# Both attentions of a small transformer layer, on one core: each pair of heads begins with a plain score step of the next pair, and the shift is turned ahead of the small value product

## What is computed

```python
def blocked_causal_attention(q, k, v, scale, cum_log_f=None):
    ...
        s = jnp.einsum('bqhd,bkhd->bhqk', q_blk, k, preferred_element_type=jnp.float32) * scale
        if use_decay:
            s = s + fq[..., :, None] - f_bh[:, :, None, :]
        ...
        s = jnp.where(mask[None, None], s, NEG)
        p = jax.nn.softmax(s, axis=-1)
        return jnp.einsum('bhqk,bkhd->bqhd', p.astype(v.dtype), v)

def attention_mixer(h, ...):
    ...
    q = rope_tail(rms_norm(q, g_q_mla), cos, sin)
    k = rope_tail(rms_norm(k, g_k_mla), cos, sin)
    o_mla = blocked_causal_attention(pad_front(q), pad_front(k), pad_front(v_mla), MLA_QK ** -0.5)[:, PAD:]
    ...
    o_fox = blocked_causal_attention(pad_front(qf), pad_front(kf), pad_front(vf), FOX_DIM ** -0.5, cum_log_f)[:, PAD:]
    return jnp.concatenate([o_mla, o_fox], axis=-1) @ w_out
```

## Time and profile before

| | |
|---|---|
| median of 3 runs | 1785.78 us (1784.84 to 1786.84) |
| the profiled execution's own time | 1785.57 us |
| its span | 1783.8 us |
| mean granted TensorE clock | 0.976 |
| the two attentions, with the MLA projections between them | 141 to 341.7 us |

### The profile page before, as it was taken

How to read it: one execution, slowest core, us unless ns; L and a number is a source line. 1 busy time by engine, 2 the same in 40 slices (tenths; PEclk the granted TensorE clock), 3 DMA queues, 4 the chain that set the end, 5 groups by cost and what they waited for, 6 DMA issues and landing times.

```text
span 1783.8 us, 27270 instructions
## 1 busy us (share of the span) xinstructions
PE 1732.7 (97%) x11417; PEld 1505.6 (84%) x11417; DVE 885.8 (50%) x1193; ACT 633.5 (36%) x980; POOL 142.9 (8%) x151
## 2 busy tenths in 40 slices
PE   7999999999999999999999999999999999879998
PEld 6997767899999999999887888888877886667987
DVE  5534556464343434655665343434665476525362
ACT  4523444433231313221233232323344465542222
POOL 1000000040000000400031000000330000003100
PEclk9999999999999999999999999999999999967999
DMA  5240000022222222222222232322464660001001
GB/s 180 71 96 8 7 26 24 25 95 95 95 95 81 86 92 94 95 95 94 94 86 95 92 99 92 98 91 98 94 88 67 99 95 4 1 11 48 1 24 71
DMA packets 137545, 129.57 MB, mean 73 GB/s; under 512 B 17633, under 2 KB 135512, under 8 KB 137452
## 3 DMA queue, kind: packets, MB, share of 16 engines
q1 hardware_dynamic: 137250, 128.18, 26.2%
q10 hardware_dynamic: 202, 0.06, 0.0%
HBM read 126.14 MB, written 2.10 MB: 72 GB/s over the span
## 4 chain that ended last, share of the span: by engine, by line
PE 92%; ACT 3%; DVE 3%; issue 1%; SPq 1%; POOL 0%; DMA 0%; ACTq 0%; DVEq 0%; POOLq 0%
PE ps L430 71%; PE ps L859 3%; PE ps L756 1%; PE ps L1094 1%; PE ps L739 1%; PE ps L1880 1%; PE ps L2140 1%; PE ps L2150 1%; PE ps L2147 1%; PE ps L1159 1%; PE ps L2167 0%; PE ps L2175 0%; PE ps L764 0%; PE ps L2098 0%; PE ps L2100 0%
## 5 line engine op out<-in xcount | busy, mean ns | idle before, releaser
L403 ACT ACTIVATE w_hi<-raw 128x1024 fp32r<-128x1024 f32 (+1 forms) x227 | 239.3, 1055 | 818.9 <-PE ps L430 812.9
L430 PE MATMUL ps<-x_hi,w_hi 128*128 128x258 f32 (+4 forms) x1640 | 450.5, 327 | 3.7 <-DVE x_lo L450 2.8
L430 PE MATMUL ps<-x_lo,w_hi 128*128 128x258 f32 (+4 forms) x1640 | 444.3, 323 | 0.0
L430 PE MATMUL ps<-x_hi,w_lo 128*128 128x258 f32 (+4 forms) x1640 | 443.4, 323 | 0.0
L411 DVE TENSOR_TENSOR w_lo<-raw,w_hi 128x1024 fp32r<-128x1024 f32 (+1 forms) x227 | 294.7, 1299 | 98.6 <-ACT w_hi L403 98.5
L430 PEld LDWEIGHTS ps<-x_hi,w_hi 128*128 128x128 f32 (+2 forms) x1640 | 273.4, 188 | 34.7 <-issue 3.8
L430 PEld LDWEIGHTS ps<-x_lo,w_hi 128*128 128x128 f32 (+2 forms) x1640 | 272.3, 187 | 28.0 <-issue 2.4
L430 PEld LDWEIGHTS ps<-x_hi,w_lo 128*128 128x128 f32 (+2 forms) x1640 | 272.2, 188 | 25.8
L430 PE MATMUL ps<-a_hi,w_hi 128*128 128x258 f32 (+1 forms) x1024 | 281.0, 325 | 3.5 <-issue 3.2
L430 PE MATMUL ps<-a_hi,w_lo 128*128 128x258 f32 (+1 forms) x1024 | 280.9, 325 | 0.0
L430 PE MATMUL ps<-a_lo,w_hi 128*128 128x258 f32 (+1 forms) x1024 | 280.6, 325 | 0.0
(11 more groups left out here) (397 smaller groups left out, 1842.5 us busy)
## 6 DMA issues: line engine op xcount, KB each, us to landing
raw<-in_w_mlp_up SPq DMA_DIRECT2D x32, 1024.0 KB, 5.4
raw<-in_w_mlp_down SPq DMA_DIRECT2D x32, 1024.0 KB, 4.8
raw<-in_w_in SPq DMA_DIRECT2D x16, 1024.0 KB, 8.9
raw<-in_w_in_conv SPq DMA_DIRECT2D x12, 1024.0 KB, 5.1
raw<-in_w_in_attn SPq DMA_DIRECT2D x8, 1024.0 KB, 5.2
raw<-in_w_out_attn SPq DMA_DIRECT2D x4, 1024.0 KB, 4.9
raw<-in_w_out_conv SPq DMA_DIRECT2D x4, 1024.0 KB, 4.8
raw<-in_w_out SPq DMA_DIRECT2D x4, 1024.0 KB, 5.7
```

The costliest lines, as they stand in the source:

```text
L403: act.activation(dst, panel_view(p)[:, :, o:o + w], ACT.Copy).then_inc(w_hi_ok, 1)
L430: ins = pe.matmul(pair_of_banks[t % 2][0:m, b, 0:c], w[:, k, :], x[:, k, x0:x0 + c], start=(k == order[0] and n == 0), stop=(k == order[-1 ...
```

## The change

Only the list of steps on PE changes, in `fox_ring`, for pairs 1 to 3 and 4 to 7. Each pair begins with step 3 of the next pair's plain scores instead of its own turned step 0. All plain steps move ahead by one place. `lat` moves from behind the turned step 1 to behind the turned step 2. `bq` and `bk` keep their places behind turned steps 1 and 2, but what stands three places ahead of each changes. The turned step 3 moves behind `sm`, and `nt` comes ahead of `pm`. No instruction is added or taken away. The order on DVE, ACT, POOL and SP stays as it is.

```diff
     for c in range(1, 4):
-        body = [("u", c, 0), ("s", c + 1, 3), ("u", c, 1), ("lat", c - 1), ("s", c + 1, 2), ("u", c, 2), ("s", c + 1, 1), ("u", c, 3),
-                ("s", c + 1, 0), ("sm", c + 1), ("pm", c), ("nt", c + 1), ("pv", c)]
+        body = [("s", c + 1, 3), ("u", c, 0), ("s", c + 1, 2), ("u", c, 1), ("s", c + 1, 1), ("u", c, 2), ("lat", c - 1), ("s", c + 1, 0), ("sm", c + 1),
+                ("u", c, 3), ("nt", c + 1), ("pm", c), ("pv", c)]
         out += [x for x in body if x[1] < (2 if x[0] == "lat" else 4)]
...
     for c in range(4, 8):
-        body = [("u", c, 0), ("s", c + 1, 3), ("u", c, 1), ("bq", c + 2), ("s", c + 1, 2), ("u", c, 2), ("bk", c + 2), ("s", c + 1, 1), ("u", c, 3),
-                ("s", c + 1, 0), ("sm", c + 1), ("pm", c), ("nt", c + 1), ("pv", c)]
+        body = [("s", c + 1, 3), ("u", c, 0), ("s", c + 1, 2), ("u", c, 1), ("bq", c + 2), ("s", c + 1, 1), ("u", c, 2), ("bk", c + 2), ("s", c + 1, 0),
+                ("sm", c + 1), ("u", c, 3), ("nt", c + 1), ("pm", c), ("pv", c)]
         out += [x for x in body if x[1] < 8]
```

## The result

| | before | after |
|---|---|---|
| median of 4 runs each | 1785.86 us (1784.84 to 1786.84) | 1830.69 us (1829.28 to 1832.21) |
| profiled execution, own time | 1785.57 us | 1830.77 us |
| its span | 1783.8 us | 1829.0 us |
| mean granted TensorE clock | 0.976 | 0.961 |
| output projection begins at | 341.68 us | 386.56 us |

The changed kernel is slower: 1.0251 times the time before, 95% interval 1.0233 to 1.0269. That lies above the range of 1804 to 1826 us.

The account below looks back on a forecast made before the run. PE, busy for 1732.7 of 1783.8 us, was taken to bound the kernel. The base of 1785.6 plus 21.8 of waits plus 8.5 of slow clock gave 1816 us, range 1804 to 1826.

Parts of the forecast that it names:

- All eleven waits: Pairs 1, 2, 4, 5 and 6: PE waits for late readers, 1.3 to 4.2 us each; 21.8 us net together.
- Point 5, the tail: End of each pair, `nt` ahead of `pm`, turned step 3 behind `sm`: saves 0.1 us a pair, costs nothing.
- the clock's term: Behind the new waits in the attentions: TensorE's granted clock falls to half in more stretches, costing 8.5 us.
- Upper bound: one for each of the eleven less the three of now, 8 x 1.7 = 14 us: Attentions: at most one slow stretch of 1.7 us cost per new wait, less the three existing ones; 14 us.
- the five taken from under it: Five more slow stretches, one in pair 2, two in pair 4, two in pair 5: 8.5 us.
- The clock falls at every one of the new waits: Rival, attentions: PE at half clock for much of each pair, 1821 us, up to 1826; chance 0.24.
- the one row of 1.24 us: Stretch 201.00 to 204.40, PE idle for 1.24 us: kept full clock, taken as sign against a fall at short waits.
- The waits without more slow clock: Rival, attentions: the new waits cost only their length, 1807 us, within 1803 to 1811; chance 0.20.
- The faster rival: Turned step 1 of each pair: slots come free in time, old waits and slow stretches go, 1777 us; chance 0.02.

Follow-up runs that it names:

- the tail alone: Kernel before with only turned step 3 moved behind `sm` and `nt` ahead of `pm`, in all pairs: 1787.05 us.
- the half-filled kernel: Changed kernel with each of the eleven waits filled to about a half with 2 to 9 unread matmuls of 512 columns: 1814.35 us.
- the reordered kernel: Changed kernel with DVE's maxima moved ahead, ACT's exponents ahead of the weights, and pair 4 beginning with its own turned step: 1780.61 us.
- the kernels with 14 and with 28 unread matmuls: The reordered kernel with unread matmuls at three waits ahead of pair 4: 14 of 512 columns, 1789.45 us; 28 of 256 columns, 1779.35 us.

## Why the prediction was wrong

**Right: the direction and the waits.** All eleven waits came, at their steps and for the readers named. By groups: the maximum of step 3 ahead of turned step 1, forecast 2.1 twice and 1.3 twice, measured 1.98 twice, 1.10 and 1.09; `sm` for the exponent, forecast 4.2 and 3.1, measured 4.05 and 2.92; the start of pair 4, forecast 1.0 + 2.0, measured 3.02; the steps behind `bq` and `bk`, forecast 2.5 and 2.2 twice, measured 2.37 and 2.11, and 2.37 and 2.10. Forecast net 21.8, measured 21.3 for the waits that the forecast names, 20.4 for all of PE's. The forecast's sum is itself 0.5 too low: it takes off 0.5 in pair 4 and again in pair 5 for old waits and the tail, where the rows have 0.3 once beside the shift's 1.0, over which the 2.0 of pair 4 was already counted; with its 0.1 a pair for the tail it would have been 22.3. The two kernels with other orders on DVE and ACT show that the readers named are the ones waited for: each took away its own waits, all of them and no other. Part of the small overestimates is the handover: 0.1 us was taken, 0.05 is seen.

**Point 5, the tail.** 0.1 a pair was taken, too little to be measured; the tail alone left every wait as it was and made no difference, so no run shows the 0.1.

**Wrong: the clock's term.** The step that failed is "Upper bound: one for each of the eleven less the three of now, 8 x 1.7 = 14 us", and with it the five taken from under it. The price was nearly right: 24.5 us over 17 more stretches of 3.4 us is 1.4 us each, where 1.7 was taken. The count was not. One wait was given one slow stretch at most, and the trace has 20 for the eleven: up to three on end, 174.5 to 184.7, 311.0 to 321.2, 341.8 to 352.0. What was called an upper bound was none. The row that could have warned was there: two stretches in a row at 272.70. It was used for a rival's upper end alone, 5 us above its 1821, and so the range ended at 1826. Had two stretches been allowed for each of eleven, the bound would have been 22 - 3 = 19 more, 32 us, and the range would have reached to 1840.

The second error is in the reason for the five: a wait's length was taken to decide. "A wait of 1.8 us, or two close ones, has brought a fall, and one of 1.2 has not" does not hold as a rule. In the changed kernel the wait of 1.10 us that ended at 329.26 was followed by a fall of the clock at 331.5, before the next wait, of 2.37 us, began at 332.40; with ACT reordered, two single waits of 1.98 us were followed by none. The long slow times come where waits stand near each other, in the MLA pairs above all, and around the wait of 4.05 us. Filling shows that the waits cause it. Which of them will, and for how long, stays open; the half-filled kernel, which was to tell, came out between the two expectations.

**The rivals.** "The clock falls at every one of the new waits" was the nearest, 1821 to 1826, and still too low by 5 to 10 us, for the same reason. The rule cited beside it, from the Trainium skill, TensorE: Matmul & The Clock Gate, "A second HAM failure mode: psum-queue depth-cycling", fits what happened here: short idle times between groups of matmuls on rotating banks, a clock that goes down and up, 68.0 us of it at 0.50. The forecast weighed the one row of 1.24 us against it and gave it too little. "The waits without more slow clock", 1807, is nearly the kernel with the waits filled, 1805.85. The faster rival fell at the place named: the maximum of step 3 ended 5.3 us after the turn, as before. But the reordered kernel, where the readers do keep pace, is 5.5 us (0.31%) faster than the kernel before, where the rival gave 8.7.

## What to carry to other kernels

When PE's order is turned over rotating slots, list for each step whose slot it takes and when that reader's own queue lets it read; that gave eleven waits to within about 0.2 us each from the trace of before. Then count waits twice on a kernel that is bound by PE: once for their length, and once for the clock. Here the clock cost about as much again (24.5 us beside 20.4), with several waits of 1 to 4 us near each other. Move the readers in the same edit: the same list on PE cost 2.5% with the old orders on DVE and ACT, and gained 0.3% together with new ones (pair 4's first two steps apart). Whether the new orders alone would give that gain was not tested.

## What the runs showed of the hardware that was not expected

- Slow clock goes on through a dense group of waits, over the work between them: up to 20.5 us at 0.50 on end (313.3 to 333.8, with ACT reordered), in which PE was busy for 16.0 us.
- The same waits do not always bring the same clock. Behind the wait of 0.80 us at 141 the kernel before and all others not named here stayed at full clock, the changed one had 3.4 us at half, the reordered one 10.2. Behind a wait of 1.24 us near 199 the kernels with 14 and with 28 unread matmuls, alike until there, had none and 3.4 us. The tail alone, with the same waits as before, had 17.0 us of slow clock instead of 10.2. Equal kernels differ from run to run by several us, and the clock goes with it: of 23 runs of the kernel before on one chip the fastest, 1780.30 us, has a mean granted clock of 0.983, the slowest, 1790.55 us, one of 0.973.
- Work that nobody reads can pay: 28 matmuls more made the kernel before faster by 0.21% (0.09% to 0.32%), and 100 more made the changed kernel 24.8 us faster (one run).
- The number of PE instructions ahead of a loop can cost time in the loop: 87 instead of 69 packets of instructions, and 6.8 us of waits in 560 to 680 us, for 14 matmuls more; with twice as many at the same places, none. That the packets cause the waits is argued from their times, not shown.
